# The first loads, first weights and input squares of a two-layer streaming encoder step, put in another order

## What is computed

```
h = rmsnorm(x, norm1_g)                       # x * rsqrt(mean(x*x) + 1e-6) * g
q_r,k_r,v_r,g_r,q_d,k_d,v_d,ga,gb = split(h @ w_in)
o_r = retention(q_r,k_r,v_r)                  # 4 heads, chunks of 64
lam = exp(sum(lambda_q1*lambda_k1)) - exp(sum(lambda_q2*lambda_k2)) + lam_init
o_d = softmax attention of 8 heads, p1 - lam*p2
x = x + (sigmoid(ga)*(norm(o_r)*silu(g_r) @ w_branch_a) + sigmoid(gb)*(norm(o_d) @ w_branch_b)) @ w_out
x = x + (silu(conv_g) * conv_a of rmsnorm(x, norm2_g) @ w_up) @ w_down
```

## Time and profile before

| what | value |
|---|---|
| median of 3 runs | 2148.88 us (2148.58 to 2149.99) |
| the profiled execution | 2149.45 us |
| its span, first to last instruction | 2147.6 us |
| PE busy | 2129.7 us (99% of the span) |
| DVE / ACT / POOL busy | 1208.3 / 971.0 / 869.9 us |
| moved by DMA | 191.63 MB |

### The profile page before, as it was taken

One profiled execution on the slowest core, in us unless ns is written; L12 is line 12 of the kernel. 1 busy time (PEld: TensorE's weight loads), 2 busy tenths in 40 slices (PEclk: granted clock), 3 DMA queues, 4 the chain that ended last, 5 costly groups with the idle time before them and its releaser, 6 DMA issues.

```text
span 2147.6 us, 43316 instructions
## 1 busy us (share of the span) xinstructions
PE 2129.7 (99%) x17624; PEld 2067.4 (96%) x17624; DVE 1208.3 (56%) x2115; ACT 971.0 (45%) x1874; POOL 869.9 (41%) x386
## 2 busy tenths in 40 slices
PE   7999999999999999999999999999999999999999
PEld 7999999999999999999999999999999999999999
DVE  6676666656355662366266576766663555613651
ACT  5655564445223452354246655544542244423441
POOL 4344423235434443433463354323353434344334
PEclk9999999999999999999999999999999999999999
DMA  5323222222222222321323233222222222222223
GB/s 178 100 86 114 75 83 79 67 92 79 80 98 79 97 69 82 104 94 61 108 90 104 77 104 100 67 67 94 83 81 79 83 95 80 81 88 99 98 66 107
DMA packets 75255, 191.63 MB, mean 89 GB/s; under 512 B 7633, under 2 KB 28721, under 8 KB 75057
## 3 DMA queue, kind: packets, MB, share of 16 engines
q1 hardware_dynamic: 66560, 182.41, 25.5%
q10 hardware_dynamic: 8496, 6.45, 0.9%
HBM read 175.41 MB, written 13.42 MB: 88 GB/s over the span
## 4 chain that ended last, share of the span: by engine, by line
PE 93%; DVE 4%; ACT 1%; issue 0%; DMA 0%; POOL 0%; DVEq 0%; ACTq 0%
PE ps L653 13%; PE ps L651 13%; PE ps L652 13%; PE ps L700 6%; PE ps L701 6%; PE ps L702 6%; PE ps L1091 4%; PE ps L1090 4%; PE ps L1092 4%; PE ps L679 2%; PE ps L723 2%; PE ps L837 2%; PE ps L871 2%; PE ps L805 2%; PE ps L797 2%; PE ps L799 1%
## 5 line engine op out<-in xcount | busy, mean ns | idle before, releaser
L516 POOL TENSOR_TENSOR wlo<-raw,whi 128x1024 fp32r<-128x1024 f32 (+1 forms) x328 | 768.7, 2362 | 1051.2 <-ACT whi L1151 1051.2
L651 PE MATMUL ps<-hl,whi 128*128 128x272 f32 x2432 | 703.4, 289 | 0.0
L653 PE MATMUL ps<-hl,wlo 128*128 128x272 f32 x2432 | 700.8, 288 | 0.0
L652 PE MATMUL ps<-hl,whi 128*128 128x272 f32 x2432 | 698.8, 287 | 0.0
L651 PEld LDWEIGHTS ps<-hl,whi 128*128 128x128 f32 x2432 | 458.6, 189 | 0.1
L653 PEld LDWEIGHTS ps<-hl,wlo 128*128 128x128 f32 x2432 | 457.6, 188 | 0.0
L652 PEld LDWEIGHTS ps<-hl,whi 128*128 128x128 f32 x2432 | 457.3, 188 | 0.1
L1151 ACT ACTIVATE whi<-raw 128x1024 fp32r<-128x1024 f32 (+1 forms) x330 | 314.2, 998 | 204.8 <-PE ps L1092 180.2
L700 PE MATMUL ps<-whi,hl 128*128 128x256 f32 x1216 | 346.8, 285 | 0.7 <-POOL wlo L516 0.6
L701 PE MATMUL ps<-wlo,hl 128*128 128x256 f32 x1216 | 343.0, 282 | 0.0
L702 PE MATMUL ps<-whi,hl 128*128 128x256 f32 x1216 | 342.5, 282 | 0.0
(11 more groups left out here) (248 smaller groups left out, 3266.3 us busy)
## 6 DMA issues: line engine op xcount, KB each, us to landing
raw<-in_w_units_dram SPq DMA_DIRECT2D x260, 512.0 KB, 4.7
raw<-in_w_down_units_dram SPq DMA_DIRECT2D x64, 352.0 KB, 3.4
kcT<-in_cache_k_dram SPq DMA_DIRECT2D x16, 256.0 KB, 3.0
out_new_k_prompt_dram<-rawk SPq DMA_DIRECT2D x8, 512.0 KB, 3.0
out_new_v_prompt_dram<-vd SPq DMA_DIRECT2D x8, 512.0 KB, 3.6
raw<-in_w_first_dram SPq DMA_DIRECT2D x6, 512.0 KB, 4.8
vc_n<-in_cache_v_dram SPq DMA_DIRECT2D x8, 256.0 KB, 4.6
vc_n<-in_cache_v_dram ACTq DMA_DIRECT2D x8, 256.0 KB, 2.7
```

What stands on the lines that cost most here:

```text
L516: e.tensor_tensor(wlo[:, s, a:b], raw[:, s, a:b], whi[:, s, a:b].bitcast(F32), ALU.subtract).then_inc(*S.up("w_ready", ("lo", j, part)))
L651: e.matmul(out, wh, hi, start=(c == 0), stop=False)
L652: e.matmul(out, wh, lo, start=False, stop=False)
L653: ins = e.matmul(out, wl, hi, start=False, stop=(c == KC - 1))
```

## The change

1. SP now issues, in this order: gains, x chunks 0 to 3, the quarters 2 and 3 of the first weights, x chunks 4 to 7, lambdas, other parameters, tables, D's unit. ACT issues only quarters 0 and 1 of the first weights.
2. The first weights are loaded, rounded and given their remainder in quarters of 512 columns (two chunks each); PE waits for a quarter before chunks 0, 2, 4 and 6 in layer 0.
3. In layer 0 ACT squares into `mer`, a buffer that holds all eight chunks, so no square waits for DVE; four squares are put between the roundings. DVE adds pairs of chunks in three sums of 1088 columns and one last of 544, in place of seven of 544. The first of the three stands between chunks 5 and 6.
4. The lambda products stand ahead of the third pair sum. The exponentials on ACT and `layer_lambda` on DVE stand behind the query evictions and the sample sum of S. (This holds in both layers.)

```diff
+        def first_weights(S, e, q):
+            a, b = q * UNIT // 4, (q + 1) * UNIT // 4
+            e.dma_start(raw[:, 0, a:b], A["w_first"][0, :, a:b]).then_inc(*S.up(f"first{q}", "in", n=16))
...
-            for c in range(0, KC, 2):
+            e.dma_start(par[:, :, 0:NVEC], A["params"][:, :, 0:NVEC]).then_inc(*S.up("gains", "in", n=16))
+            for c in range(KC):
                 e.dma_start(x[:, c, :], A["x"][c]).then_inc(*S.up(f"x_in{c}", "x", n=16))
-                if c < 4:
-                    a = c * UNIT // 4
-                    e.dma_start(raw[:, 0, a:a + UNIT // 2], A["w_first"][0, :, a:a + UNIT // 2]).then_inc(*S.up(f"first{c // 2}", "in", n=16))
+                if c == 3:
+                    for q in (2, 3):
+                        first_weights(S, e, q)
             e.dma_start(prob[:, :, 0:4 * DIFF_HD], A["lambdas"]).then_inc(*S.up("lambdas", "in", n=16))
+            e.dma_start(par[:, :, NVEC:], A["params"][:, :, NVEC:]).then_inc(*S.up("params", "in", n=16))
+            e.dma_start(small[:, :], A["tab_small"]).then_inc(*S.up("tables", "in", n=16))
...
                     for c in range(KC):
-                        weights(0, c)
+                        if l:
+                            weights(0, c)
+                        elif c % 4 == 0:
+                            e.wait_ge(*S.at("first_lo", k=c // 4 - 1))
+                        elif c % 4 == 2:
+                            e.wait_ge(*S.at("w_ready", k=c // 4 - 1))
...
+            def first_square(c):
+                e.activation(mer[:, c, :], x[:, c, :], ACT.Square).then_inc(*S.up("sq_ready", ("sq", c)))
...
                 norm_hi(c, part, vecs[:, 0, c:c + 1])
-                if c in (0, 2):
-                    hi("P", 0, c // 2)
-            for c, part in CUT:
-                norm_square(c, part)
+                for q in {0: (0,), 1: (1,), 3: (2, 3)}.get(c, ()):
+                    first_hi(q)
+                if c in (0, 1, 3, 4):
+                    first_square(c - c // 3)
+            for c in range(4, KC):
+                first_square(c)
...
                 norm_lo(c, part, vecs[:, 0, c:c + 1])
-                if c in (0, 2):
-                    first_lo(c // 2)
+                for q in {0: (0,), 1: (1,), 3: (2, 3)}.get(c, ()):
+                    first_lo(q)
+                if c == 5:
+                    first_sum(1)
             normed_samples()
-            for c, part in CUT:
-                if c and part != 0:
-                    norm_sum(c, part)
-
+            first_sum(2)
             e.wait_ge(*S.at("lambdas", "in"))
...
+            first_sum(3)
+            e.wait_ge(*S.own())
+            e.tensor_tensor(acc[:, :], mer[:, 0, :], mer[:, 1, :], ALU.add).then_inc(*S.up("acc_ready"))
```

More of the change, by code:

```diff
@@ L731, in pe_program @@
             e.wait_ge(*S.at("pool_step", "one"))
-            for _ in S.layers():
+            for l in S.layers():
                 for _ in S.bodies("S"):
@@ L1140, in hi @@
                 if part == 0:
[L1141 to L1149, removed]
+                    if j >= 2:
+                        e.wait_ge(*S.at("mm_ready", ("end", j - 2)))
+                    else:
+                        e.wait_ge(*S.at("mm_ready", k=0))
+                    e.wait_ge(*S.at(f"raw{s}", k=32 * (j // 2 + 1)))
                 a, b = (0, n // 2) if part == 0 else (n // 2, n)
@@ L1155, in prep, with first_hi @@
                 hi(phase, j, 1)
+            def first_hi(q):
+                a, b = q * UNIT // 4, (q + 1) * UNIT // 4
+                e.wait_ge(*S.at(f"first{q}", "in"))
+                e.activation(whi[:, 0, a:b], raw[:, 0, a:b], ACT.Copy).then_inc(
+                    *(S.up("hi_ready", ("hi", 0, q // 2)) if q % 2 else S.up("first_hi", q)))
             def rest_copy(bank, key, prev, scaled=True, ready="mm_ready", buf=rest):
@@ L1191, in act_program @@
             S.prime("hi_ready", 1)
[L1192 to L1196, removed]
+            first_weights(S, e, 0)
+            first_weights(S, e, 1)
             S.prime("st_ready", 1)
@@ L1211, in act_program @@
                     hi("S", 1, 1)
-                    e.wait_ge(*S.at("lam_ready", k=0))
-                    e.activation(lam_exp[:, :], lam_sum[:, :], ACT.Exp).then_inc(*S.up("act_step", key="lexp"))
                     e.wait_ge(*S.at("rs_ready", "rstd"))
@@ L1219, in act_program @@
                     rest_copy(S_BANKS[NT], ("N", 0, NT), None)
+                    e.wait_ge(*S.at("lam_ready", k=0))
+                    e.activation(lam_exp[:, :], lam_sum[:, :], ACT.Exp).then_inc(*S.up("act_step", key="lexp"))
                 for p in S.bodies("D"):
@@ L1700, in norm_sum, with first_sum, first_lo @@
                 e.tensor_tensor(acc[:, :], acc[:, :], sq[:, c % 2, :], ALU.add).then_inc(*S.up("acc_ready", ("acc", c)))
-            def first_lo(part):
-                h = slice(part * UNIT // 2, (part + 1) * UNIT // 2)
-                e.wait_ge(*S.at("hi_ready", ("hi", 0, part)))
+            def first_sum(k):
+                e.wait_ge(*S.at("sq_ready", ("sq", 2 * k + 1)))
+                e.wait_ge(*S.own())
+                e.tensor_tensor(mer[:, 0:2, :], mer[:, 0:2, :], mer[:, 2 * k:2 * k + 2, :], ALU.add).then_inc(*S.up("dve_step"))
+            def first_lo(q):
+                h = slice(q * UNIT // 4, (q + 1) * UNIT // 4)
+                e.wait_ge(*(S.at("hi_ready", ("hi", 0, q // 2)) if q % 2 else S.at("first_hi", q)))
                 e.tensor_tensor(wlo[:, 0, h], raw[:, 0, h], whi[:, 0, h].bitcast(F32), ALU.subtract).then_inc(
-                    *S.up("w_ready", ("lo", 0, part)))
+                    *(S.up("w_ready", ("lo", 0, q // 2)) if q % 2 else S.up("first_lo", q)))
             def normed_samples():
@@ L1782, in dve_program @@
                     norm_mean("mm1")
-                    layer_lambda(l)
                     e.wait_ge(*S.at("rs_ready", "rstd"))
@@ L1788, in dve_program @@
                     sample_sum(rawq[0:DEC, NT, :], S_BANKS[NT], ("N", 0, NT), "q")
+                    layer_lambda(l)
+                    e.wait_ge(*S.own())
                 def sum_of_sample(head, sem, key):
```

## The result

The change makes the kernel **slower by 0.45%**: 2158.47 us (median of 6 runs) against 2148.73, ratio 1.0045 with a 95% interval of 1.0036 to 1.0055. The forecast was 2149.6, no change, with 2151.6 as the upper end. So 9.7 us have to be explained, and about 9 of them were not in the sum. The profiled execution took 2158.64 us with a span of 2156.8, against 2149.45 and 2147.6.

The account below looks back on a forecast made before the run. PE was taken as the bound, busy without a break from 45 us, so only the start could win. -0.1 plus 0.8 for the clock gave 0.7 us later: 2150.2 profiled, 2149.6 against the median, range 2145.0 to 2151.6.

Parts of the forecast that it names:

- the mark: Chunk 4 of D's first tile on PE, at 31.22 before; forecast 31.15 plus 0.8 for the clock, without waiting for POOL.
- The early start: PE's first matmul at 7.3 instead of 12.7; the 5.4 us are lost in front of `stats`, 0.1 left.
- the 9.7 by the row of the gains: Far end for quarter 0's landing on ACT's queue, where the gains took 7.9 us; 5.8 was taken.
- I take 0.8: PE after idling 21.1 to 27.4 starts at the slow spacing; cost 0.8 us, bounds 0 and 1.3.
- At no cost: Lambda work behind the evictions may wait up to 2.4 us twice, covered; 1 us lost if the cover is thinner.
- In layer 1 nothing ahead of S changes: Claim about layer 1, closing the part on costs; no time was entered for it.
- -0.1 as forecast: Layer 0, before the clock's cost: the mark at 31.15 instead of 31.22, 0.1 us left of the earlier start.
- the 3.73 that I had put together: Layer 0, PE from the sums over partitions to the mark: 12 matmuls (1.4) and 2.33 us.
- ACT's queue late: Start loads: quarter 0 lands at 9.7, mark 4.1 later plus 0.8, 2153.8 us; chance 0.10, half beyond the bound.
- Rival 1: Layer 0: DVE's sums get ahead of POOL, mark 1.9 to 3.1 earlier, 2147.8 to 2145.8 us; chance 0.28.

Follow-up runs that it names:

- run 3: The changed kernel with POOL's phase S subtractions held until the last sum of squares (`acc`) is ready: 2159.71 us, ratio 1.0050.
- run 8: The kernel before, its order of loads kept, with only the eight-chunk buffer of squares and the pair sums: 2151.90 us, ratio 1.0015.
- run 1: The changed kernel with the exponentials and `layer_lambda` back at their old places: 2152.17 us, ratio 1.0014.
- run 2: The kernel before with only the lambda move (exponentials behind the query evictions, `layer_lambda` behind the sample sum): 2161.86 us, ratio 1.0061.
- run 7: The kernel before with only the new load order and weights in quarters; old squares buffer, seven sums, lambda work at old places: 2145.17 us, ratio 0.9985.
- run 10: The kernel of run 5 with lambda products behind the last sum, plus 10 matmuls on zeros before PE's first wait: 2146.21 us, against 2146.05 without them.
- run 5: The changed kernel with POOL held until the sum of squares is ready and the late lambda work back at its old place: 2146.73 us, ratio 0.9993.
- run 4: The changed kernel with 30 unread matmuls on PE ahead of layer 0's statistics: 2157.59 us, ratio 1.0046.

## Why the prediction was wrong

**What held.** D's unit landed at 19.07 (forecast 19.1); both lambda products were held by POOL's subtractions, and the last two sums stood behind the products; `acc` was ready at 27.6 (27.3); no wait for POOL at the mark. The early start was given back in front of the sums over partitions, as forecast, and run 3 shows that POOL is the reason. The wide buffer, which was entered as a relief for ACT, brings POOL's start among DVE's sums (run 8), and the sum had that right. How much of the delay of `acc` is the wide buffer's and how much comes from the products ahead of the last sums, no run separates.

**What was a little off.** Quarter 0 landed near 6.5, not 5.8, and the first matmul came at 8.0, not 7.3. From there to the sample products PE took 14.2 us and not 12.7, because the slow start lasted 6 us and not 2.7. It mattered little: `acc` decided. The 5.8 stood beside what the Trainium skill says ("DMA: Bandwidth & Descriptors", section "Issuing engines are not separate DMA queues"), that issuing from several engines only saves issuing time; it was nearer than the 9.7 by the row of the gains.

**First failed step: the clock.** "I take 0.8", from bounds of 0 and 1.3. The upper bound itself was wrong. It was taken from the 12 slow matmuls of the start and carried over as it stood. Behind the idle time the half clock lasted 6.75 us, and everything in it was slow: the sums over partitions took 2.28 for 1.38 us, 13 sample products 1.89 us (1.03 in the kernel before), and 12 matmuls of D 2.7 for 1.7. From the start of the sums to the mark are 6.75 us, where the kernel before needed 31.22 - 26.60 - 0.63 = 3.99. So the term is 2.8, not 0.8. The Trainium skill ("TensorE: Matmul & The Clock Gate", section "HAM oscillation — how this bites in real kernels") says that a long wait between bursts puts the engine back to the low clock. The trace agrees: behind the wait of 4.4 us the granted clock is 0.50.

**Second failed step: "At no cost".** It priced the late lambda work at nothing because PE had no wait in this stretch, and at 1 us "if that cover is thinner". It named what delays the work, POOL's subtractions, "up to 2.4 us twice", and that is what came (2.33 and 1.97). It did not ask who waits for DVE behind it. The answer is PE's third key tile, through `osum_done`, and the list of waits of the kernel before already had a small row at this place, among the weight loads, which no part of the prediction took up:

```profile
PEld ps L700 <- DVEq L220: 0.2, 1, 0.2
```

It cost 3.8 us, and 2.6 us of half clock behind it. "In layer 1 nothing ahead of S changes" is true of what is ahead of S, and hid that the lambda work moves in both layers. Runs 1 and 2 show this step by itself: 6.3 us in the changed kernel, 13.2 in the kernel before.

**The sum, mended.** At the mark: -0.1 as forecast, + 0.3 because the sums started at 27.73 instead of 27.4, + 0.3 because the stretch from there to the mark takes 3.99 us at full clock and not the 3.73 that I had put together, + 2.8 for the clock: 3.3, as measured (34.48 - 31.22). Layer 1: 3.8 for the wait and 2.6 for the clock, read from the matched matmuls, and 0.5 won back later. Together 9.2, the difference of the two spans. The two steps that failed are thus 2.0 us of the clock term and 6.4 us of the work priced at nothing.

**The rivals.** None came about. The slow one, ACT's queue late, was the wrong mechanism for the right sign. Rival 1 (DVE ahead of POOL) did not come from luck in the landings, but it is what run 7 brings about by keeping the old buffer: its mark is at 28.19, where that rival had 28.1 plus the clock. The change thus contains a kernel that is 3.4 us faster than the one before; parts 3 and 4 turn that into 9.7 us of loss.

**What stays open.** Behind waits of 1.6 us and more every trace shows a slow stretch. Behind shorter ones it comes in some executions and not in others of the same kernel: the traces of runs 7 and 10 show one behind 1.04 and 0.43 us, that of run 5 none behind 0.60, while the mean granted clocks have it the other way round, below 1.000 in eight of ten executions of run 5 and in one of ten of run 7. What besides the idle time decides was not settled, nor whether the light work behind the wait has a part in it. Why two executions of run 4 took 2160 us and more is open too.

## What to carry to other kernels

Before moving small work later on an engine, look for every signal that this engine gives behind it, increments without arithmetic included, and ask whether the moved instructions can meet a long POOL instruction there: the price here was the length of POOL's instruction, not their own. A wait that looks like waste may be what keeps two engines out of each other's way; check what starts earlier when it goes. And price an idle stretch of PE by the time it stands still plus the half-clock stretch behind it, which here cost 2.8 and 2.6 us in the two places, and 1.4 us in run 2 behind a wait as long as the second.

## What the runs showed of the hardware

- A 128 x 1 TENSOR_TENSOR of DVE, 0.16 us by itself, lasts 2.33 us when it meets a 2.4 us subtraction of POOL. The size of the DVE instruction gives no protection. DVE instructions with one input kept their length in the middle of a subtraction: a TENSOR_REDUCE of 0.29 us at 22.79 and a COPY of 0.14 us at 1105.01.
- It goes both ways: beside DVE's pair sums POOL's two subtractions took 6.24 instead of 4.7 to 4.8 us (run 8).
- PE's half clock came back after as little as 0.43 us (run 10) and 1.04 us (run 7, in one of ten executions) of idleness followed by the sums over partitions and the sample products, for about 3 us, while the 12.7 us of idleness at the start were followed by 2.7 us of slow spacing in the kernel before and 8.0 us of it by 6 us in the changed one. The length of the slow stretch doesn't follow the idle time. Nor does its cost: behind the same 3.67 us in layer 1 it was 2.6 us in the changed kernel and 1.4 us in run 2.
- At the start the granted clock reads 1.00 while the matmuls are 0.216 us apart; only in run 10, where PE had worked before, does it read 0.50 there. In the first microseconds of a trace the spacing tells more than the clock.
